# A triangular inverse kept as compact 32x32 diagonal blocks in the RWKV-7 stage of a decoder trunk

## The chip, the core and the metric

The kernel runs on one core of a Trainium2 chip. Its engines are TensorE (PE in the profile; PEld is its weight load), VectorE (DVE), ScalarE (ACT), GpSimd (POOL) and SyncE (SP, which issues most DMAs). The metric is the device time of one execution in microseconds.

## The reference

Two decoder layers run over a prompt of 256 tokens and over 8 sample tokens, each with an FFN, a mixer of three parallel groups (RWKV-7, a short convolution, Mamba-2), and another FFN. The change is in the RWKV-7 group, whose recurrence per head is

```python
def step(S, inp):
    r_t, w_t, k_t, v_t, kk_t, b_t = inp
    Sa = jnp.einsum('bhij,bhj->bhi', S, -kk_t)
    S = S * w_t[:, :, None, :] + Sa[..., None] * b_t[:, :, None, :] + v_t[..., None] * k_t[:, :, None, :]
    return S, jnp.einsum('bhij,bhj->bhi', S, r_t)
```

for 16 heads of width 64. The kernel computes it for the prompt in chunks of 64 tokens. Within a chunk the rank-one updates depend on one another through a strictly triangular 64x64 matrix N, so that a chunk needs the inverse of I - N (signs as the kernel takes them). The 8 sample tokens take one plain step each.

## The kernel before

`back_stage` does this part once in each of the two layers. Two heads lie on the 128 partitions, so there are 8 head pairs (RT = 8). With 4 chunks there are 8 triangular 64x64 matrices to a pair: 4 along the free axis (index q) in each partition half.

A hand-written software pipeline runs over steps g = 0 to 9. In step g the pair g gets its products (`gram`, then `mask` on DVE, and on POOL `first_done`, the first level of the inverse), the pair l = g - 1 gets its inverse, and the pairs c = g - 2 and p = g - 3 get `solve`, `transfer`, `own_outputs`, `own_states`, `chunk`, and the mean and variance. Each engine runs its own list in program order. Semaphores join the lists: nothing else sets the order.

The inverse is grown by doubling. X (`x`, tile `inverse`) and its transpose (`xt`, tile `inverse_t`) are right for diagonal blocks of size b, and a level makes them right for 2b: `levels` masks the off-diagonal blocks of N (`level` on POOL, tile `n_levels`), TensorE forms T1 = N_b X (`level_t1`), ACT copies T1 from PSUM (`t1_copy`, tile `n_x`), TensorE forms X T1 and its transpose (`level_u`, two products), and DVE adds both to `x` and `xt` (`update`). The levels are 2, 4, 8, 16 and 32, and the last needs only the transpose. A product here (`blocks`) is 8 matmuls of a 64x64 weight block with 64 columns, in fp32; the trace has two records for each fp32 matmul, 16 to a product. The halves of the partitions are separate array tiles. Before level 0 DVE adds the identity to `xt` (`start`), TensorE transposes it (`turn_x`), and ACT copies that to `x` (`x_copy`). `solve` uses `xt` as the weights.

DVE also runs the eight instructions of the sample step (`step`), two to `mask` the next pair, `transfer`, `centre` and `gated`. In the last steps PE and DVE take work for the output projection as well (`short`, `ws.split_lo`). The lists between them are those of the functions below.

## Time and profile before

| | |
|---|---|
| median of 3 runs | 1665.74 us (1665.28 to 1670.03) |
| span of the profiled execution | 1667.1 us |
| granted TensorE clock, mean over the span | 0.983 |
| PE busy | 1566.2 us (94%) |
| DVE busy | 1140.1 us (68%) |
| ACT busy | 858.5 us (51%) |
| POOL busy | 262.7 us (16%) |
| back_stage's loop in layer 0 (g = 0 to 9), roughly | 441 to 597 us |
| the same in layer 1, roughly | 1261 to 1419 us |

The profile is of one execution, and no time of its own stands beside its span; the span is 1.4 us above the median of the runs. A busy share says how long an engine had at least one instruction in flight: matmuls overlap, so PE can be at 94% and still have room.

### The profile page before, as it was taken

The page shows a single profiled execution, that of the slowest core. Times are in us where ns is not written, and L with a number is a line of the kernel's source. Part 1 is how long each engine was busy: PE and PEld are TensorE (multiplying, and loading weights), DVE is VectorE, ACT ScalarE, POOL GpSimd, SP SyncE. Part 2 cuts the span into 40 slices and gives each one's busy share as a digit, 9 for nine tenths or more (in the row PEclk, how much of TensorE's full clock was granted, in tenths as well). Part 3 has the DMA queues.
Part 4 walks back from the last instruction along what each step waited for, and adds up shares of the span by engine and source line. Part 5 has one row for each costly group of instructions (what it writes and reads, how often), then busy time and mean ns, then how long its engine had stood idle before and what let it go on. Part 6 is the DMA issues. An engine that isn't in the chain of part 4 may idle for free. (4 is left out here: it accounts for less than half of the span.)

```text
span 1667.1 us, 41414 instructions
## 1 busy us (share of the span) xinstructions
PE 1566.2 (94%) x17379; PEld 1486.8 (89%) x17379; DVE 1140.1 (68%) x1822; ACT 858.5 (51%) x1515; POOL 262.7 (16%) x259
## 2 busy tenths in 40 slices
PE   7999999989799899999999999999997989899997
PEld 6999999987688789999999999989775878799997
DVE  6565587795798667665575656968768886676654
ACT  5444464667444555444354444657673445554443
POOL 0000003001356431000000000030014554300000
PEclk9999999999899999999999999999998999999999
DMA  7555556471244545555454655644703463455552
GB/s 230 178 172 170 168 159 199 130 208 53 59 125 120 144 157 161 194 179 186 143 186 160 194 183 175 189 141 128 215 1 102 126 178 98 131 189 187 183 178 71
DMA packets 280650, 256.28 MB, mean 154 GB/s; under 512 B 48054, under 2 KB 268700, under 8 KB 280450
## 3 DMA queue, kind: packets, MB, share of 16 engines
q1 hardware_dynamic: 276698, 252.05, 48.5%
q8 instruction: 139, 2.28, 0.6%
q10 hardware_dynamic: 3768, 1.59, 0.4%
q14 instruction: 45, 0.37, 0.1%
HBM read 242.22 MB, written 11.38 MB: 152 GB/s over the span
## 5 line engine op out<-in xcount | busy, mean ns | idle before, releaser
L209 ACT ACTIVATE front_hi<-front_raw 128x1024 fp32r<-128x1024 f32 (+2 forms) x230 | 238.5, 1039 | 262.0 <-PE ps L234 255.5
L216 DVE TENSOR_TENSOR front_lo<-front_raw,front_hi 128x1024 fp32r<-128x1024 f32 (+1 forms) x210 | 252.2, 1201 | 109.0 <-ACT front_hi L209 108.2
L209 ACT ACTIVATE out_hi<-out_raw 128x1024 fp32r<-128x1024 f32 (+1 forms) x168 | 173.3, 1038 | 219.1 <-PE ps L234 205.1
L216 DVE TENSOR_TENSOR out_lo<-out_raw,out_hi 128x1024 fp32r<-128x1024 f32 (+1 forms) x148 | 183.9, 1243 | 108.1 <-ACT out_hi L209 107.3
L232 PE MATMUL ps<-front_h_hi,front_hi 128*128 128x264 f32 (+1 forms) x816 | 241.3, 296 | 4.9 <-DVE front_lo L216 3.3
L234 PE MATMUL ps<-front_h_hi,front_lo 128*128 128x264 f32 (+1 forms) x816 | 233.0, 286 | 0.0
L233 PE MATMUL ps<-front_h_lo,front_hi 128*128 128x264 f32 (+1 forms) x816 | 232.7, 285 | 0.0
L232 PE MATMUL ps<-ffn_h_hi,out_hi 128*128 128x264 f32 x704 | 200.7, 285 | 0.1
L233 PE MATMUL ps<-ffn_h_lo,out_hi 128*128 128x264 f32 x704 | 200.0, 284 | 0.0
L234 PE MATMUL ps<-ffn_h_hi,out_lo 128*128 128x264 f32 x704 | 199.8, 284 | 0.0
L232 PE MATMUL ps<-in_h_hi,front_hi 128*128 128x264 f32 x688 | 197.4, 287 | 0.0
L234 PE MATMUL ps<-in_h_hi,front_lo 128*128 128x264 f32 x688 | 196.5, 286 | 0.0
L233 PE MATMUL ps<-in_h_lo,front_hi 128*128 128x264 f32 x688 | 196.5, 286 | 0.0
L232 PEld LDWEIGHTS ps<-front_h_hi,front_hi 128*128 128x128 f32 (+1 forms) x816 | 154.1, 189 | 13.5 <-issue 12.7
L233 PEld LDWEIGHTS ps<-front_h_lo,front_hi 128*128 128x128 f32 (+1 forms) x816 | 154.2, 189 | 0.7
L234 PEld LDWEIGHTS ps<-front_h_hi,front_lo 128*128 128x128 f32 (+1 forms) x816 | 153.5, 188 | 0.1
L216 POOL TENSOR_TENSOR front_lo<-front_raw,front_hi 128x1024 fp32r<-128x1024 f32 (+1 forms) x20 | 50.1, 2504 | 543.9 <-ACT front_hi L209 543.9
L232 PEld LDWEIGHTS ps<-ffn_h_hi,out_hi 128*128 128x128 f32 x704 | 132.7, 189 | 0.4 <-ACT ffn_h_hi L283 0.2
L233 PEld LDWEIGHTS ps<-ffn_h_lo,out_hi 128*128 128x128 f32 x704 | 132.7, 188 | 0.1
L234 PEld LDWEIGHTS ps<-ffn_h_hi,out_lo 128*128 128x128 f32 x704 | 132.6, 188 | 0.0
L233 PEld LDWEIGHTS ps<-in_h_lo,front_hi 128*128 128x128 f32 x688 | 131.3, 191 | 0.1
L232 PEld LDWEIGHTS ps<-in_h_hi,front_hi 128*128 128x128 f32 x688 | 131.2, 191 | 0.1
(400 smaller groups left out, 3891.7 us busy)
## 6 DMA issues: line engine op xcount, KB each, us to landing
front_raw<-in_w_in SPq DMA_DIRECT2D x50, 1024.0 KB, 5.2
out_raw<-in_ffn_w_in SPq DMA_DIRECT2D x44, 1024.0 KB, 5.2
front_raw<-in_ffn_w_in SPq DMA_DIRECT2D x40, 1024.0 KB, 5.3
back_sample_rows<-row_scratch SPq DMA_DIRECT2D x160, 128.0 KB, 3.0
out_raw<-in_w_out SPq DMA_DIRECT2D x16, 1024.0 KB, 6.3
front_raw<-in_ffn_w_out SPq DMA_DIRECT2D x16, 896.0 KB, 4.6
out_raw<-in_ffn_w_out SPq DMA_DIRECT2D x16, 896.0 KB, 4.6
front_raw<-in_ffn_w_out SPq DMA_DIRECT2D x8, 1024.0 KB, 5.0
```

Source lines behind the costliest of these rows:

```text
L209: act.activation(self.hi[n % self.RING][:, 0:k, 0:w], self._raw(n), ACT.Copy).then_inc(self.hi_ready, 1)
L216: eng.tensor_tensor(self.lo[n % self.RING][:, 0:k, 0:w], self._raw(n), self.hi[n % self.RING][:, 0:k, 0:w].bitcast(F32), ALU.subtract).the ...
L232: pe.matmul(out, hi[:, j, 0:w], x_hi[:, j], start=start and j == 0, stop=False)
L233: pe.matmul(out, hi[:, j, 0:w], x_lo[:, j], start=False, stop=False)
L234: mm = pe.matmul(out, lo[:, j, 0:w], x_hi[:, j], start=False, stop=stop and j == k - 1)
```

## The change

`x` now holds only the diagonal 32x32 blocks, one to each of the four partition quadrants, so a tile is 128x128 in place of 128x256. There are four levels (2 to 16) that work on these blocks, and a last step for the off-diagonal 32x32 block (LT = 5 steps in all). The products of the four levels (`small_blocks`) are 16 matmuls of a 32x32 weight block with 32 columns, on the four diagonal 32x32 tiles of the array. The transpose is no longer updated by a product of its own. After each change of `x`, DVE writes the transpose of each 32x32 block to `x_t` (`turn_blocks`), and waits for its own addition before. The last step is two half products (8 matmuls each). `finish` on DVE writes the right half of `xt`, `upper_blocks` on ACT the left half. `turn_x` no longer waits for DVE; DVE's addition of the identity (`start`) has moved from the middle of a step to its end and reads PSUM, and ACT's `x_copy` is gone. POOL loses one of five `level` operations a pair and gains one memset a layer.

```diff
--- before.py
+++ after.py
@@ -45,7 +45,8 @@
...
 LN_SCALE = 2.0 ** 20
-LEVELS = (2, 4, 8, 16, 32)
+LEVELS = (2, 4, 8, 16)
+HB = 32
 ROWS_A = (("norm_mix", 8), ("norm_ffn2", 8), ("rwkv_mu", 27), ("rwkv_w0", 8), ("rwkv_a0", 8),
@@ -77,6 +78,8 @@
...
     parts["levels"] = np.concatenate([level_t(b) for b in LEVELS], 1) * 1.0
+    parts["eye32"] = (i[:, None] % HB == np.arange(HB)[None, :]) * 1.0
+    parts["sides"] = np.stack([i % C < HB, i % C >= HB], 1) * 1.0
     t = np.arange(T)
...
@@ -1585,7 +1588,7 @@
-    LV, V = len(LEVELS), 5
+    LV, LT, V = len(LEVELS), len(LEVELS) + 1, 5
     KK, DEC, MB, KEY, REC = range(V)
...
@@ -1601,7 +1604,7 @@
...
         lev = st.sb("n_levels", [P, 2, 4, C])
-        x = st.sb("inverse", [P, 2, 4, C])
+        x, x_t = st.sb("inverse", [P, 2, 4, HB]), st.sb("inverse_blocks_t", [P, 2, 4, HB])
         xt = st.sb("inverse_t", [P, 3, 4, C])
...
@@ -1626,7 +1629,10 @@
...
         first, levels = env.const("first"), env.const("levels")
+        eye32, sides = env.const("eye32"), env.const("sides")
         half = (slice(0, C), slice(C, P))
+        quarter = tuple(slice(i * HB, (i + 1) * HB) for i in range(4))
+        in_block = (slice(0, HB), slice(HB, C))
         sin = d["state_rwkv_wkv"][layer].rearrange("b (m h) i j -> m (h i) b j", h=2)
...
@@ -1748,6 +1754,7 @@
...
                     pool.tensor_tensor(short_lo[:, c], mix.ys[:, c], short_hi[:, c].bitcast(F32), ALU.subtract).then_inc(s("short_lo"), 1)
+                pool.memset(t1[:, :, HB:C], 0.0).then_inc(s("t1_zeroed"), 1)
                 for g in range(RT + 1):
...
@@ -1770,7 +1777,6 @@
...
                     if l >= 0:
-                        level(l, 4)
                         key_row(l)
...
@@ -1800,15 +1806,15 @@
...
                 def t1_copy(p, i):
-                    n = LV * p + i
+                    n = LT * p + i
                     act.wait_ge(s("t1_ps"), n + 1)
                     if n:
-                        act.wait_ge(s("ut_ps"), n)
-                    act.activation(t1[:].rearrange("p q t -> p (q t)"), ps[:, T1B, 0:4 * C], ACT.Copy).then_inc(s("t1_in"), 1)
-
-                def x_copy(p):
-                    act.wait_ge(s("x_ps"), p + 1)
-                    act.activation(x[:, p % 2].rearrange("p q t -> p (q t)"), ps[:, T1B, 0:4 * C], ACT.Copy).then_inc(s("x_in"), 1)
+                        act.wait_ge(s("u_ps"), n)
+                    act.activation(t1[:, :, 0:HB], ps[:, T1B, 0:4 * HB].rearrange("p (q t) -> p q t", q=4), ACT.Copy).then_inc(s("t1_in"), 1)
+
+                def upper_blocks(p):
+                    act.wait_ge(s("xt_in"), LT * (p + 1))
+                    act.activation(xt[:, p % 3, :, 0:HB], x_t[:, p % 2], ACT.Copy, scale=sides[:, 0:1]).then_inc(s("upper_in"), 1)
                 def rv_copy(p):
...
@@ -1944,6 +1950,7 @@
...
                         t1_copy(l, 4)
+                        upper_blocks(l)
                         rv_copy(l)
...
@@ -1954,8 +1961,6 @@
...
                         shift_store(6)
-                    if g < RT:
-                        x_copy(g)
                     if c >= 0:
...
@@ -1999,24 +2004,28 @@
...
                                       cau[:].unsqueeze(1).to_broadcast([P, 4, 2 * C]), ALU.mult).then_inc(s("masked"), 1)
+                four = lambda b: ps[:, b, 0:4 * HB].rearrange("p (q t) -> p q t", q=4)
+                flat = lambda a: a.rearrange("p q t -> p (q t)")
+
+                def turn_blocks(p):
+                    dve.transpose(flat(x_t[:, p % 2]), flat(x[:, p % 2])).then_inc(s("xt_in"), 1)
+
                 def start(p):
-                    dve.wait_ge(s("first_done"), p + 1)
-                    dve.tensor_tensor(xt[:, p % 3], xt[:, p % 3], eye2.unsqueeze(1).to_broadcast([P, 4, C]),
-                                      ALU.add).then_inc(s("start"), 1)
+                    dve.wait_ge(s("x_ps"), p + 1)
+                    dve.tensor_tensor(x[:, p % 2], four(T1B), eye32.unsqueeze(1).to_broadcast([P, 4, HB]), ALU.add).then_inc(s("x_in"), 1)
+                    dve.wait_ge(s("x_in"), p + 1)
+                    turn_blocks(p)
                 def update(p, i):
-                    four = lambda b: ps[:, b, 0:4 * C].rearrange("p (q t) -> p q t", q=4)
-                    if i < LV - 1:
-                        dve.wait_ge(s("u_ps"), (LV - 1) * p + i + 1)
-                        if i:
-                            dve.wait_ge(s("x_up"), (LV - 1) * p + i)
-                        else:
-                            dve.wait_ge(s("x_in"), p + 1)
-                        dve.tensor_tensor(x[:, p % 2], x[:, p % 2], four(UB), ALU.add).then_inc(s("x_up"), 1)
-                    dve.wait_ge(s("ut_ps"), LV * p + i + 1)
-                    if i:
-                        dve.wait_ge(s("xt_up"), LV * p + i)
-                    dve.tensor_tensor(xt[:, p % 3], xt[:, p % 3], four(UB + 1), ALU.add).then_inc(s("xt_up"), 1)
+                    dve.wait_ge(s("u_ps"), LT * p + i + 1)
+                    dve.tensor_tensor(x[:, p % 2], x[:, p % 2], four(UB), ALU.add).then_inc(s("x_up"), 1)
+                    dve.wait_ge(s("x_up"), LV * p + i + 1)
+                    turn_blocks(p)
+
+                def finish(p):
+                    dve.wait_ge(s("u_ps"), LT * (p + 1))
+                    dve.scalar_tensor_tensor(out=xt[:, p % 3, :, HB:C], in0=x_t[:, p % 2], scalar=sides[:, 1:2], in1=four(UB + 1),
+                                             op0=ALU.mult, op1=ALU.add).then_inc(s("xt_up"), 1)
                 def transfer(p):
...
@@ -2105,8 +2114,6 @@
...
                         gated(p)
-                    if g < RT:
-                        start(g)
                     if g < 4:
...
@@ -2118,9 +2125,11 @@
...
                         step(l, 5)
-                        update(l, 4)
+                        finish(l)
                         step(l, 6)
                         step(l, 7)
+                    if g < RT:
+                        start(g)
                     if g == RT - 1:
...
@@ -2183,39 +2192,52 @@
...
                     mm.then_inc(s("g_ps"), 1)
-                def blocks(at, left, right):
+                def small_blocks(at, left, right):
                     for q in range(4):
-                        for w in half:
-                            mm = pe.matmul(ps[w, at, q * C:(q + 1) * C], left[w, q], right[w, q], start=True, stop=True)
+                        for i, w in enumerate(quarter):
+                            mm = pe.matmul(ps[w, at, q * HB:(q + 1) * HB], left(w, q, in_block[i % 2]), right(w, q), start=True, stop=True)
                     return mm
                 def turn_x(p):
-                    pe.wait_ge(s("start"), p + 1)
+                    pe.wait_ge(s("first_done"), p + 1)
                     if p:
-                        pe.wait_ge(s("t1_in"), LV * p)
-                    for q in range(4):
-                        for w in half:
-                            mm = pe.matmul(ps[w, T1B, q * C:(q + 1) * C], xt[w, p % 3, q], eye2[w], start=True, stop=True)
-                    mm.then_inc(s("x_ps"), 1)
+                        pe.wait_ge(s("t1_in"), LT * p)
+                    small_blocks(T1B, lambda w, q, c: xt[w, p % 3, q, c], lambda w, q: eye32[w]).then_inc(s("x_ps"), 1)
                 def level_t1(p, i):
                     n = LV * p + i
-                    pe.wait_ge(s("lev_done"), n + 1)
                     if i:
-                        pe.wait_ge(s("x_up"), (LV - 1) * p + i)
-                        pe.wait_ge(s("t1_in"), n)
+                        pe.wait_ge(s("x_up"), n)
+                        pe.wait_ge(s("t1_in"), LT * p + i)
                     else:
                         pe.wait_ge(s("x_in"), p + 1)
-                    blocks(T1B, lev[:, n % 2], x[:, p % 2]).then_inc(s("t1_ps"), 1)
+                    if i < LV:
+                        pe.wait_ge(s("lev_done"), n + 1)
+                        mm = small_blocks(T1B, lambda w, q, c: lev[w, n % 2, q, c], lambda w, q: x[w, p % 2, q])
+                    else:
+                        for q in range(4):
+                            for o in range(2):
+                                top, low = quarter[2 * o], quarter[2 * o + 1]
+                                mm = pe.matmul(ps[low, T1B, q * HB:(q + 1) * HB], gm[top, p % 3, q, 0, HB:C], x[top, p % 2, q],
+                                               start=True, stop=True)
+                    mm.then_inc(s("t1_ps"), 1)
                 def level_u(p, i):
-                    n = LV * p + i
-                    pe.wait_ge(s("t1_in"), n + 1)
-                    if n:
-                        pe.wait_ge(s("xt_up"), n)
-                    if i < LV - 1:
-                        blocks(UB, xt[:, p % 3], t1[:]).then_inc(s("u_ps"), 1)
-                    blocks(UB + 1, t1[:], xt[:, p % 3]).then_inc(s("ut_ps"), 1)
+                    pe.wait_ge(s("t1_in"), LT * p + i + 1)
+                    pe.wait_ge(s("xt_in"), LT * p + i + 1)
+                    if i < LV:
+                        mm = small_blocks(UB, lambda w, q, c: x_t[w, p % 2, q], lambda w, q: t1[w, q, 0:HB])
+                    else:
+                        if p == 0:
+                            pe.wait_ge(s("t1_zeroed"), 1)
+                        else:
+                            pe.wait_ge(s("xt_up"), p)
+                        for q in range(4):
+                            for o in range(2):
+                                low = quarter[2 * o + 1]
+                                mm = pe.matmul(ps[half[o], UB + 1, q * HB:(q + 1) * HB], t1[low, q], x_t[low, p % 2, q],
+                                               start=True, stop=True)
+                    mm.then_inc(s("u_ps"), 1)
                 def gv(p):
@@ -2235,7 +2257,8 @@
                 def solve(p):
-                    pe.wait_ge(s("xt_up"), LV * (p + 1))
+                    pe.wait_ge(s("xt_up"), p + 1)
+                    pe.wait_ge(s("upper_in"), p + 1)
                     pe.wait_ge(s("rv_in"), p + 1)
```

In TensorE's list, the second half of step g = 3 (pair l = 2, from the products behind T1 of the fourth level). `back_inverse,back_n_levels` or `back_inverse,back_products` is a T1, L2299 and L2304 are `chunk`, L2232 is `gv`, L2198 before is `turn_x`. Before:

```order
L2189 MATMUL ps<-back_n_x,back_inverse_t 64x64 x8
L2189 MATMUL ps<-back_inverse_t,back_n_x 64x64 x8
L2299 MATMUL ps<-back_read_out,back_states 64x64 x2
L2304 MATMUL ps<-back_states,back_carry 64x64 x2
L2189 MATMUL ps<-back_inverse,back_n_levels 64x64 x8
L2232 MATMUL ps<-back_tok,back_products 64x64 x8
L2299 MATMUL ps<-back_read_out,back_states 64x64 x2
L2304 MATMUL ps<-back_states,back_carry 64x64 x2
L2189 MATMUL ps<-back_inverse_t,back_n_x 64x64 x8
L2198 MATMUL ps<-cst,back_inverse_t 64x64 x8
```

The same stretch of TensorE's list now (L2322 and L2327 are `chunk`, L2254 is `gv`):

```order
L2198 MATMUL ps<-back_n_x,back_inverse_blocks_t 32x32 x16
L2322 MATMUL ps<-back_read_out,back_states 64x64 x2
L2327 MATMUL ps<-back_states,back_carry 64x64 x2
L2221 MATMUL ps<-back_inverse,back_products 32x32 x8
L2254 MATMUL ps<-back_tok,back_products 64x64 x8
L2322 MATMUL ps<-back_read_out,back_states 64x64 x2
L2327 MATMUL ps<-back_states,back_carry 64x64 x2
L2238 MATMUL ps<-back_inverse_blocks_t,back_n_x 64x32 x8
L2198 MATMUL ps<-cst,back_inverse_t 32x32 x16
```

The order of the work is the same. Of the two products behind a T1 one is gone, the others have twice the matmuls at a quarter of the size, and tiles of 32 and of 64 now alternate.

In DVE's list, the end of step g = 4 and the begin of the next, before (`back_prod` and the rows with `back_sample` are the sample step, `back_products` the masks):

```order
L2015 TENSOR_TENSOR back_inverse<-back_inverse,ps 128x256
L2019 TENSOR_TENSOR back_inverse_t<-back_inverse_t,ps 128x256
L2068 SCALAR_TENSOR_TENSOR gate_211<-xs,cols,gate_211 128x264
L2004 TENSOR_TENSOR back_inverse_t<-back_inverse_t,cst 128x256
L2052 TENSOR_TENSOR back_sample_wkv<-back_sample_wkv,back_outer 128x512
L2019 TENSOR_TENSOR back_inverse_t<-back_inverse_t,ps 128x256
L2055 TENSOR_TENSOR back_prod<-back_sample_wkv,back_sample_rows 128x512
L2057 TENSOR_REDUCE xs<-back_prod 128x8
L1998 TENSOR_TENSOR back_products<-ps,cst 128x512 x2
```

and now:

```order
L2021 TENSOR_TENSOR back_inverse<-back_inverse,ps 128x128
L2011 STREAM_TRANSPOSE back_inverse_blocks_t<-back_inverse 128x128
L2077 SCALAR_TENSOR_TENSOR gate_211<-xs,cols,gate_211 128x264
L2061 TENSOR_TENSOR back_sample_wkv<-back_sample_wkv,back_outer 128x512
L2027 SCALAR_TENSOR_TENSOR back_inverse_t<-back_inverse_blocks_t,cst,ps 128x4x32
L2064 TENSOR_TENSOR back_prod<-back_sample_wkv,back_sample_rows 128x512
L2066 TENSOR_REDUCE xs<-back_prod 128x8
L2015 TENSOR_TENSOR back_inverse<-ps,cst 128x128
L2011 STREAM_TRANSPOSE back_inverse_blocks_t<-back_inverse 128x128
L2003 TENSOR_TENSOR back_products<-ps,cst 128x512 x2
```

`start` (L2004 before, L2015 and L2011 now) stands behind the whole sample step, right ahead of the masks of the next pair.

In step g = 0, DVE's list before:

```order
L2004 TENSOR_TENSOR back_inverse_t<-back_inverse_t,cst 128x256
L2112 SCALAR_TENSOR_TENSOR bonus_212<-bonus_212,cols,gate_211 128x264 x2
L2117 SCALAR_TENSOR_TENSOR y_short<-y_short,cols,sc_root_219 128x264 x3
L1998 TENSOR_TENSOR back_products<-ps,cst 128x512 x2
L2015 TENSOR_TENSOR back_inverse<-back_inverse,ps 128x256
```

and now, with five vector operations ahead of `start`:

```order
L2119 SCALAR_TENSOR_TENSOR bonus_212<-bonus_212,cols,gate_211 128x264 x2
L2124 SCALAR_TENSOR_TENSOR y_short<-y_short,cols,sc_root_219 128x264 x3
L2015 TENSOR_TENSOR back_inverse<-ps,cst 128x128
L2011 STREAM_TRANSPOSE back_inverse_blocks_t<-back_inverse 128x128
L2003 TENSOR_TENSOR back_products<-ps,cst 128x512 x2
```

Here `start` has moved behind `bonus` and `y_short`, and both of its instructions work on 128 elements in place of 256.

## Rows read from the trace of the kernel before

**Rows 1.** The page's head, part 1 and the clock line of part 2.
```profile
span 1667.1 us, 41414 instructions
...
PE 1566.2 (94%) x17379; PEld 1486.8 (89%) x17379; DVE 1140.1 (68%) x1822; ACT 858.5 (51%) x1515; POOL 262.7 (16%) x259
...
PEclk9999999999899999999999999999998999999999
```

**Rows 2.** Busy us (instructions) by engine, clock, DMA; stretches are steps 2 to 7.
```profile
467.31:481.36 14.05, 12.79 (x420) 11.83 (x416) 13.48 (x26) 6.12 (x18) 9.61 (x11) 1.00 0.48 134
...
543.90:561.54 17.64, 13.75 (x394) 12.23 (x389) 13.00 (x24) 8.17 (x23) 10.85 (x10) 1.00 0.95 268
sum 94.23, PE 86.25 PEld 77.87 DVE 80.17 ACT 42.01 POOL 56.37; mean PE 14.38 PEld 12.98 DVE 13.36 ACT 7.00 POOL 9.39
```

**Rows 3.** Who waited for whom over those six steps, engines of the loop.
```profile
DVE back_inverse L2015 <- PE ps L2189: 7.2, 14, 1.6
PE ps L2189 <- issue: 4.7, 5, 2.9
```

**Rows 4.** Timeline, one level of pair 3 (start us, us, what; x counts records).
```profile
500.18 0.68 PE L2189 MATMUL ps<-back_n_x,back_inverse_t 64*64 64x64 f32 x16
500.70 0.63 PE L2189 MATMUL ps<-back_inverse_t,back_n_x 64*64 64x64 f32 x16
500.91 0.42 DVE L2015 TENSOR_TENSOR back_inverse<-back_inverse,ps 128x256 f32<-128x256 f32 x1
501.26 0.66 PE L2167 MATMUL ps<-cst,back_b_k 128*128 128x128 f32 x4
501.38 0.42 DVE L2019 TENSOR_TENSOR back_inverse_t<-back_inverse_t,ps 128x256 f32<-128x256 f32 x1
501.72 0.68 DVE L2041 TENSOR_REDUCE back_sample_sa<-back_prod 128x8 f32<-128x512 f32 x1
```

**Rows 5.** Timeline of PE, step g = 9: products whose matmuls lie on four 64x64 tiles.
```profile
591.22 0.46 PE L2275 MATMUL ps<-back_products,back_tok 64*64 64x64 f32 x16
591.50 0.41 PE L2279 MATMUL ps<-back_products,back_u_w 64*64 64x64 f32 x16
591.73 0.41 PE L2286 MATMUL ps<-back_tok 64*64 64x64 f32 x16
```

**Rows 6.** Instructions of L2189 (ns min/median/max), and groups by line of L739 and L740.
```profile
L2189 PE MATMUL ps<-back_inverse,back_n_levels x1280: 212/219/268, 449.5 to 1402.0; 64*64 64x64 f32 x183
...
L739 PE MATMUL ps<-cst,fin_squares_sum 128*128 128x1 f32 x4 | 0.5, 230 | 0.0
...
L740 PE MATMUL ps<-cst,fin_squares_sum 128*8 128x1 f32 x2 | 0.2, 168 | 0.0
```

**Rows 7.** Groups by line with shapes kept apart (count | busy us, mean ns).
```profile
L1998 DVE TENSOR_TENSOR back_products<-ps,cst 128x512 f32<-128x512 f32 x32 | 20.5, 682 | 10.9 <-PE ps L2182 10.9
...
L1216 DVE SCALAR_TENSOR_TENSOR segments<-ps,tok_cum_dt,cst 128x128 f32<-128x128 f32 x16 | 5.5, 341 | 0.0
...
L796 DVE TENSOR_TENSOR xbc_conv<-xbc_conv,outer 128x64 f32<-128x64 f32 x6 | 1.4, 225 | 0.2
```

**Rows 8.** Timeline of DVE in step g = 0 and into g = 1, layer 0.
```profile
445.39 0.89 DVE L2004 TENSOR_TENSOR back_inverse_t<-back_inverse_t,cst 128x256 f32<-128x256 f32 x1 [0.84 <-POOL back_inverse_t L1759]
...
447.86 2.67 DVE L2117 SCALAR_TENSOR_TENSOR y_short<-y_short,cols,sc_root 128x264 f32<-128x264 f32 x3
450.45 1.27 DVE L1998 TENSOR_TENSOR back_products<-ps,cst 128x512 f32<-128x512 f32 x2
```

**Rows 9.** Timeline of PE in step g = 8, after the projection's first matmuls.
```profile
571.50 0.62 PE L2189 MATMUL ps<-back_inverse,back_n_levels 64*64 64x64 f32 x14
...
582.87 1.09 PE L2243 MATMUL ps<-back_gv_a,back_inverse_t 64*64 64x128 f32 x16
```

**Rows 10.** Timeline of PE in step g = 7, a wait inside a product.
```profile
558.31 0.27 PE L2189 MATMUL ps<-back_inverse_t,back_n_x 64*64 64x64 f32 x3 [2.86 <-issue]
```

**Rows 11.** Busy time by stretch at the loop's start in layer 1.
```profile
1257.00:1273.00 16.00, 12.44 (x202) 9.76 (x204) 9.66 (x14) 7.02 (x17) 7.86 (x10) 0.79 0.45 120
```

6 lines of the change are left out of this document (3 added, 3 removed).

## The prediction

> **What bounds the kernel now.** I read the page first: the span is 1667.1 us, PE is busy for 94% of it and its clock is granted almost throughout [rows 1]. The chain that ended last is PE nearly everywhere, which says little about a pipelined loop, so I went on to the stage that the change touches and cut it at the first mask of each pipeline step. Six steps, g = 2 to 7, take 94.23 us, 15.7 each; in a step PE is busy for 14.38, DVE for 13.36, ACT for 7.0 and POOL for 9.4 [rows 2]. So two engines are close to the bound and neither is it alone. The list of waits says the same: in six steps DVE waits 7.2 us for PE ahead of `x`'s update, and PE waits 4.7 us for "issue", 2.9 of it in one place [rows 3, 10]. The two in-order lists interlock. Relief of one engine alone is worth less than it measures; here both get some, of unequal size, and a step should shrink by an amount between the two.
>
> **PE's products.** A product of 16 records starts 0.52 us after the one ahead of it (500.18 and 500.70) [rows 4]; I take 0.5. A pair has 15: one for `turn_x`, five T1, four for `x`, five for `xt`, so 7.5 us. One record lasts 0.22 [rows 6], so the other 15 start within 0.68 - 0.22 = 0.46, 31 ns apart, on two array tiles: 62 ns between records on one tile. Products that use four tiles start 0.28 and 0.23 apart [rows 5], 16 ns a record, again some 62 ns on one tile. So a tile accepts a record about every 62 ns when it has 64 columns behind a 64-wide weight, tiles work side by side, and records can be issued 16 ns apart at least. Does a tile's pace shrink with the size? Four records with 128-wide weights and one column took 0.50, two with 8-wide weights 0.20, of which the last record is 0.17 (the mean) [rows 6]: 0.03 apart. So it shrinks, down to 0.03 at least. A 32x32 record has half the columns and half the weights: I take 31 ns a tile. A small product is 32 records on four tiles, 8 rounds, 0.25 us. The bounds: 0.25 below, since nothing shows a tile under 30 ns, and above 32 x 31 ns = 1.0, if they got only the pace of the two-tile products. A choice of 0.5 would be the 16 ns a record that four tiles do show. I take 0.25 because the tile, and not the issue, sets the pace in both rows that I have.
>
> A pair then has nine small products (2.25), a T1 of 16 records on two tiles (0.25) and a last product whose weights are 64 wide (0.5): 3.0 in place of 7.5, 4.5 us less.
>
> **Changes of tile size.** The last record of the product that starts at 500.70 starts at 501.33 - 0.22 = 501.11, the first 128x128 record at 501.26: 0.15 later, where inside a product it is 0.03 [rows 4]. The first record behind a change is also 0.05 longer (268 against 219) [rows 6]. I take 0.15 for a change. From PE's list, a step now changes between 64 and 128 six times; after the change every product of the inverse stands between others, and there are 21 changes. Fifteen more cost 2.25 us. Net, PE gets 2.25 us a step back. The Trainium skill (TensorEngine Tiling (Array Packing), Key Properties) says that a change of tiling mode drains the engine. The trace agrees with 0.15 us, and with a free change the relief would be 4.5.
>
> **DVE.** The update of `x` holds DVE for 0.47 (500.91 to 501.38) and that of `xt` for 0.34 (to 501.72) [rows 4]; three levels at 0.81, one at 0.66 (I take 0.33 for each operation where no wait splits them), the last `xt` and `start` at 0.34 each make 3.8 us. Now there are five additions of 128 elements, each awaited by the transpose behind it, five transposes, and `finish`. A 64-element operation takes 0.225 and a 256-element one 0.42, so 128 elements 0.29; with the semaphore 0.32 for the awaited one and 0.21 for one followed by a stranger (0.08 less than its duration, as 0.34 against 0.42). `finish` is like the 128-element operation from PSUM at 0.341, 0.26 in the queue [rows 4, 7]. That is 5 x 0.53 + 0.26 = 2.9, so 0.9 less. No row shows a block transposition. Below, it can't beat 0.225 (saving 0.3 more a pair); above I take the 512-element mask, 0.68, which costs 5 x 0.39 = 1.95 more and turns the 0.9 into a loss of 1.05. I take 0.29, since it moves the same elements as the addition beside it. The Trainium skill (VectorE: DVE Perf Modes, The three transpose paths) gives 311 ns for 128x128 in bf16, an estimate for fp32 of 0.31; no run here shows it, and it would change the sum by 0.1.
>
> **The order.** The transpose is off the chain of a level: T1 needs only `x`, and T1 with ACT's copy (0.45 and 0.4) covers the 0.32 until `x_t` is there. ACT has room for `upper_blocks` [rows 2]. `start` now ends a step. PE then waits with `level_t1(l, 0)`, and behind it in its list stand `solve`, so `uw_copy` and `transfer`, and `level_u`. But PE has `turn_x`, `chunk` and `gram` (some 1.9 us) to do while DVE does `finish`, two sample instructions and `start` (some 1.9), and DVE has two masks (1.2) to do while PE catches up with T1 and `solve` (some 2). I charge 0.2 a step. In g = 0 `start` stands behind five instructions; they no longer stand behind the old `start`, its wait of 0.84 us for POOL and its 0.8 in the queue, so they end about 1.6 us before 450.45, at 448.8, early enough for the first T1 at 449.5. I count nothing there [rows 6, 8]. POOL's memset and its dropped level are off the path.
>
> **The sum.** A step gets shorter by something between DVE's 0.9 and PE's 2.25. The middle is 1.6, less 0.2 for the order: 1.4. Seven steps (g = 1 to 7) give 9.8. In g = 8 the chain of four levels from 571.50 to `solve` at 582.87 is 11.4 us [rows 9]: a level loses two times 0.25 on PE, 0.08 on ACT and 0.13 on DVE and gains two changes, 0.3, so 0.4 a level, 1.6. That is 11.4 a layer and 22.8 for both. The profile's span of 1667.1 lies 1.4 above the median of the runs, 1665.7; I subtract from the median: **1643 us**, and 1628 to 1655 for this case alone (a step 0.6 to 2.2 shorter).
>
> **Rivals.**
> - *More* (8%): DVE had its waits only because PE was late, and PE's full 2.25 comes through: 7 x 2.25 + 2.5, twice, 1629. For it speaks that DVE waits 7.2 us in six steps; against it, that DVE's busy 13.4 less 0.9 leaves 12.5.
> - *Little* (22%): the step is held by DVE's list and by the new wait at its end, where PE stands still, and it shrinks by 0.3: 7 x 0.3 + 0.8, twice, 1660. For it speaks the step of 14.05 us with DVE busy for 13.48 [rows 2].
> - *Small matmuls are dear* (9%, slower): 32x32 records get no four-way overlap and run 31 ns apart, a product costs 1.0. Then PE has 9 x 1.0 + 1.0 + 2.25 = 12.25 for 7.5, 4.75 more, of which its slack of 1.3 hides some: 3.4 a step, 16 steps, 55 us, 1720. It decides from 0.5 a product, where PE gains nothing, and certainly from 0.64. Against it speak the four-tile rows [rows 5]. The Trainium skill (same tiling page, Instruction Overhead) says that a matmul has about 60 cycles of overhead, so that 1 column costs as much as 60. Taken for records in a row, 25 ns each, that would be 0.8 a product and about 1700; rows 5, at 16 ns a record, disagree.
> - *The transposition is dear* (7%, slower): at 0.68 DVE loses 1.05 a step, about 0.6 of it in the period: 16 x 0.6, 1676. It decides from 0.47, where 5 x 0.18 eat the 0.9.
> - *The clock* (4%, slower): with sparser matmuls the granted clock falls inside the loop, as in the stretch with 0.79 after DVE and PE had little work [rows 11], which is 3.4 us of clock in 16. Eight such spells undo the gain and more: 1670. Against it: a stretch with PE busy for only 13.75 of 17.64 kept 1.00 [rows 2].
> - *As forecast* (50%).
>
> **How the numbers follow.** About 0.3%, 5 us, can be told from no change. Faster by more: 50 + 8 and a third of *little*, 66%. Within: most of the rest of *little*, 13%. Slower: 9 + 7 + 4 and 1 of *little*, 21%. The range leaves out *dear matmuls* and the far end of *more*: 1625 to 1680.
>
> **What would show it.** Right: six steps in 84 to 89 us; 32x32 products in which 32 records start within 0.3 us; `STREAM_TRANSPOSE` near 0.3; about 0.15 between a 32 and a 64 record; DVE's own busy time in a step near 12.5, PE's idle time higher, the clock at 1.00. Wrong: products of 0.5 or more, changes of 0.3 or more (15 of them then cost the whole 4.5), a transposition over 0.4, a wait of PE over 1 us at the head of each step, or a clock under 1.00 in the loop. A stall inside a product that waits for nothing the profile shows, as the 2.86 us in g = 7 [rows 10], could grow with PE's 160 matmuls a pair in place of 120; I have no price for it.

## The result, and the profile after the change

The change makes the kernel slower: 1695.16 us median of four runs (1691.84 to 1698.14) against 1666.66 of before (now four runs, 1665.28 to 1670.03), a ratio of 1.0168 with a 95% interval of 1.015 to 1.0185. The profiled execution spans 1689.8 us.

The page's head, the clock line and the queues of instruction transfers, after:

```profile
span 1689.8 us, 43864 instructions
...
PE 1554.5 (92%) x18659; PEld 1455.8 (86%) x18659; DVE 1115.5 (66%) x1838; ACT 852.7 (50%) x1515; POOL 251.3 (15%) x245
...
PEclk9999999999889799999999999999997988999999
...
q8 instruction: 149, 2.44, 0.6%
```

Against [rows 1], every engine is busy for less (PE 12 us, DVE 25, ACT 6, POOL 11) in a span that is 23 us longer. What went up is PE's instructions: 1280 MATMULs and as many weight loads. The last row is one that I had not read before the prediction: the queue that carries instructions. Its row of before:

```profile
q8 instruction: 139, 2.28, 0.6%
```

Ten transfers and 0.16 MB more for 2560 PE instructions: a transfer is 16 KB and brings a block of 256 instructions.

Busy time by stretch after, steps g = 2 to 7, in the columns of [rows 2]:

```profile
466.68:483.21 16.53, 15.11 (x520) 12.70 (x513) 11.52 (x26) 5.94 (x18) 8.35 (x10) 0.71 0.43 116
483.21:502.05 18.84, 13.68 (x529) 10.89 (x525) 13.01 (x29) 6.58 (x21) 7.88 (x10) 1.00 0.38 104
...
537.59:557.62 20.03, 16.53 (x529) 13.53 (x528) 11.57 (x25) 6.69 (x20) 7.97 (x10) 0.76 0.36 99
557.62:579.35 21.73, 14.87 (x510) 11.98 (x509) 12.41 (x25) 9.21 (x24) 10.17 (x9) 0.75 0.77 230
sum 112.67, PE 89.84 PEld 72.64 DVE 72.57 ACT 41.31 POOL 50.62; mean PE 14.97 PEld 12.11 DVE 12.09 ACT 6.89 POOL 8.44
```

Six steps take 112.67 us where they took 94.23. The second row is the one to look at: full clock, PE busy for 13.68, DVE for 13.01, and yet 18.84 us. PE's timeline in that stretch, the rows with a wait for nothing that the profile shows:

```profile
484.29 0.39 PE L2198 MATMUL ps<-back_inverse,back_n_levels 32*32 32x32 f32 x24 [1.03 <-issue]
488.64 0.45 PE L2290 MATMUL ps<-back_products,back_u_w 64*64 64x64 f32 x12 [1.19 <-issue]
492.98 0.38 PE L2198 MATMUL ps<-back_n_x,back_inverse_blocks_t 32*32 32x32 f32 x20 [1.22 <-issue]
497.48 0.33 PE L2327 MATMUL ps<-back_states,back_carry 64*64 64x64 f32 x3 [1.21 <-issue]
501.56 0.44 PE L2191 MATMUL ps<-back_a_r,back_b_k 64*64 64x128 f32 x6 [0.32 <-issue]
```

PE stops in the middle of products, of old ones (`chunk`, the state products) as of new ones, at even distances. Cut from stop to stop:

```profile
484.28:488.63 4.35, 2.98 (x125) 2.35 (x125) 1.75 (x4) 1.42 (x4) 4.09 (x6) 1.00 0.42 104
488.63:492.97 4.34, 3.12 (x126) 2.44 (x126) 3.09 (x6) 0.87 (x2) 2.74 (x4) 1.00 0.19 65
492.97:497.47 4.50, 3.29 (x127) 2.52 (x127) 3.96 (x10) 1.62 (x6) 1.05 (x1) 1.00 0.30 97
```

125 to 127 MATMUL records and as many weight loads, with a few semaphore instructions: one transfer of 256 instructions each time. PE has used up a block and the next one is not there. Over the six steps the pace is the same before and after: some 2,550 records, 20.2 blocks, in 94.23 us are 4.7 us a block, some 3,090 records, 24.5 blocks, in 112.67 are 4.6. The equal pace does not say that the supply bound the kernel before, as the runs with few rows show below. Added up over the whole span, PE's waits for "issue" are 13.8 us before the change and 40.7 after. The 26.9 us more are nearly the whole loss of 28.5.

Not every wait for "issue" is one for a block, so I also counted PE's instructions (MATMULs, weight loads and semaphore instructions) in the packed traces. A block's end falls at every 256th instruction, always at the same remainder. Of the 40.7 us, 39.1 are 37 stops of 0.1 us or more that all stand within four instructions of such an end. Before the change there are 10 such stops with 9.3 us. In the trace after, transfer number k (from 0) never starts before PE has begun 256 k + 154 instructions, and PE never gets beyond 256 k + 449 until transfer k is over. So a transfer starts only when PE has fewer than 300 instructions left. PE resumes some 2.4 us after the start of the transfer that it lacked (median of the stops in the loops), though the transfer itself takes about 1.0.

One more wait grew in these six steps. PE waits three times for `start` (DVE's L2015) at the head of a step, up to 1.5 us (us in total, times, longest):

```profile
PE ps L2198 <- issue: 12.7, 9, 2.7
PE ps L2198 <- DVE back_inverse L2015: 3.0, 3, 1.5
```

The small products and the transposition themselves, after (the instructions of one line, ns min/median/max; then groups by line; then the timeline):

```profile
L2198 PE MATMUL ps<-back_inverse,back_n_levels x2048: 184/191/258, 450.9 to 1422.0; 32*32 32x32 f32 x187
```

```profile
L2011 DVE STREAM_TRANSPOSE back_inverse_blocks_t<-back_inverse 128x128 f32<-128x128 f32 x80 | 24.9, 312 | 2.7
```

```profile
486.51 0.45 PE L2198 MATMUL ps<-back_inverse,back_n_levels 32*32 32x32 f32 x32 [0.19 <-DVE back_inverse L2021]
486.89 0.46 PE L2287 MATMUL ps<-back_tok,back_u_w 64*64 64x64 f32 x16
```

All 32 records of a product start within 0.45 - 0.19 = 0.26 us, 8 ns apart, and the next tile size starts 486.89 - 486.77 = 0.12 behind the last. (The Trainium skill, TensorEngine Tiling (Array Packing), Instruction Overhead, gives a matmul some 60 cycles of overhead, an estimate of 25 ns. If that held for records in a row, whatever their tiles, the 8 ns here would disagree; on one tile a record comes every 34 ns, and there nothing in this trace contradicts it.)

### The profile page after: what moved, and what is told of

The parts are those of the page before. It is cut to its first block and busy times, and to the rows that moved or that the text cites. A ratio compares the mean times of both kernels' runs of the same rounds, so it can differ in the third digit from the quotient of the medians.

```text
span 1689.8 us, 43864 instructions
## 1 busy us (share of the span) xinstructions
PE 1554.5 (92%) x18659; PEld 1455.8 (86%) x18659; DVE 1115.5 (66%) x1838; ACT 852.7 (50%) x1515; POOL 251.3 (15%) x245
```

## The experiments

Three theories. **Supply**: PE's instructions come in blocks of 256, and in the loop a block takes 4.3 to 4.5 us where PE has to wait for it; 530 records a step are 4.2 blocks. **Clock**: the granted clock was 0.71 to 0.82 in some steps. **Order**: `start` at the end of DVE's list. All ratios are against the kernel before, with 95% intervals.

| run | us | ratio | the inverse's matmuls a pair | instruction transfers |
|---|---|---|---|---|
| after | 1695.2 | 1.0168 (1.015 to 1.0185) | 160 | 149 |
| T1 and `turn_x` merged | 1663.4 | 0.9975 (0.9959 to 0.9991) | 120 | 139 |
| before, weights split | 1692.4 | 1.0142 (1.0122 to 1.0161) | 160 | 149 |
| before, columns split | 1701.5 | 1.0199 (1.018 to 1.0219) | 160 | 149 |
| after, filled | 1703.4 | 1.0212 (1.0186 to 1.0237) | 160 + 6 | 150 |
| before, spread waits | 1692.5 | 1.0145 (1.0129 to 1.0162) | 120 | 142 |
| before, clustered waits | 1704.8 | 1.0214 (1.0198 to 1.0229) | 120 | 144 |
| merged, filled in g = 0 to 2 | 1671.7 | 1.0025 (1.0014 to 1.0036) | 120 + 6 | 139 |
| no `turn_x` | 1659.9 | 0.9945 (0.9926 to 0.9964) | 112 | 137 |
| the same, `start` at the end | 1665.4 | 0.9988 (0.9975 to 1.0001) | 112 | 137 |
| full blocks, transposed by DVE | 1652.1 | 0.9907 (0.9891 to 0.9922) | 88 | 131 |
| the same, `start` on POOL | 1659.6 | 0.9948 (0.9935 to 0.9962) | 88 | 131 |
| after, few rows | 1680.1 | 1.0066 (1.0043 to 1.0089) | 160 | 149 |
| before, few rows | 1665.0 | 0.9973 (0.9962 to 0.9985) | 120 | 139 |
| split, few rows | 1678.2 | 1.0062 (1.0047 to 1.0077) | 160 | 149 |
| merged, few rows | 1656.3 | 0.9931 (0.9914 to 0.9948) | 120 | 139 |
| clusters, few rows | 1700.1 | 1.0189 (1.0171 to 1.0206) | 120 | 144 |

Not all of the ranges recorded before the runs held. The weight split (1692.4) and the spread waits (1692.5) came out just below the supply theory's ranges, the filled merged kernel (1671.7) and `start` on POOL (1659.6) above every range given for them. The run without `turn_x` (1659.9) came out where neither of its theories had it. With few rows, the changed, the split and the merged kernel fell between the two ranges that each had. The clustered waits and the column split came out inside the supply theory's ranges, but for reasons of their own, as said below.

### Fewer instructions for the same work

The masked levels are block diagonal in 32s, so one 64x64 weight does what two 32x32 weights do:

```diff
-                        mm = small_blocks(T1B, lambda w, q, c: lev[w, n % 2, q, c], lambda w, q: x[w, p % 2, q])
+                        for q in range(4):
+                            for w in half:
+                                mm = pe.matmul(ps[w, T1B, q * HB:(q + 1) * HB], lev[w, n % 2, q], x[w, p % 2, q], start=True, stop=True)
```

> The changed kernel, with T1 of the four levels and turn_x as 8 matmuls of a 64x64 weight (block diagonal in 32s) with 32 columns in place of 16 matmuls of 32x32: the same result, PE's time much the same, but 120 matmuls a pair as before the change, not 160. Theory A (supply): PE takes its instructions in blocks of some 126 MATMUL records with their weight loads, and a block cannot take less than about 4.35 us. A step of the changed kernel has some 530 records, 4.2 blocks, 18.3 us (the measured mean of seven steps is 18.3); with 445 it is 3.5 blocks, 15.4 us. So seven steps take 105 to 112 us in place of 128, and the time falls to 1650 to 1668. Theory B (clock): the granted clock falls in the loop because matmuls are small and sparse; they stay so, so the steps stay near 18 and the time is 1685 to 1700. Theory C (the transposition and start at the end of DVE's list): nothing of it is changed, 1690 to 1697.

(`turn_x` is merged in the same way.) 1663.4, so 32 us go with 40 matmuls a pair, more than the whole loss of 28.5. PE's waits for "issue" are 15.0 us in all, of which 13.4 at ends of blocks, 25.7 less than after the change. The steps fall to 13.9 to 17.2, two of them:

```profile
464.88:481.14 16.26, 15.32 (x440) 13.41 (x438) 11.30 (x26) 5.97 (x18) 7.56 (x10) 0.72 0.44 117
481.14:495.79 14.65, 13.66 (x449) 11.34 (x445) 12.43 (x28) 6.61 (x21) 8.83 (x10) 1.00 0.49 133
```

The edit changes one more thing: T1 now has the tile size of its neighbours, so that a step changes tile size 14.8 times in this trace, where it was 20.7 after the change (5.7 before it). Six changes fewer at 0.12 are 0.7 us of PE's time a step, at most 11 us in 16 steps. No run separates them from the 40 matmuls; the 25.7 us less at ends of blocks leave some 6 of the 32 us for them.

### The same number of instructions in the kernel before

```diff
-                    blocks(T1B, lev[:, n % 2], x[:, p % 2]).then_inc(s("t1_ps"), 1)
+                    for q in range(4):
+                        for o, w in enumerate(half):
+                            for k in range(2):
+                                to = slice(o * C + k * 32, o * C + k * 32 + 32)
+                                mm = pe.matmul(ps[to, T1B, q * C:(q + 1) * C], lev[w, n % 2, q, k * 32:k * 32 + 32], x[w, p % 2, q],
+                                               start=True, stop=True)
+                    mm.then_inc(s("t1_ps"), 1)
```

> The kernel before, with each T1 of the inverse as 16 matmuls (weights of 64x32 in place of 64x64, the same columns): nothing else is changed, but a pair has 160 matmuls, as many as after the change. Theory A: a step goes from some 445 to some 525 records, 3.5 to 4.2 blocks of 4.35 us, so 15.7 to about 18.2 us, 16 steps, 1695 to 1710, with a stall inside a product about every 126 records. Theories B and C: the full-size products, VectorE's list and start are as before; only ten more changes of tile size come in, 1.5 us of PE's time a step of which its slack hides most, so 1666 to 1680, and no stalls at even distances.

> The kernel before, with each T1 as 16 matmuls of 64x64 weights with 32 columns in place of 8 with 64: no other tile size and no new change of tile size, but each weight is loaded twice, and a pair has 160 matmuls. Theory A: as the run with weights in halves, 1695 to 1710, stalls about every 126 records. Theories B and C: 1666 if 32 columns cost half of 64, up to 1685 if a matmul costs by its weight (5 x 0.5 us a step, less PE's slack of 1.3).

The second run splits the moving columns instead (`ps[w, T1B, at:at + 32]`, `x[w, p % 2, q, k * 32:k * 32 + 32]`). 1692.4 and 1701.5, with the clock at 1.00 in every step from g = 1 to 6 and neither a transposition nor a moved `start`. Two steps of the first, and a block between two of its stops:

```profile
482.35:499.84 17.49, 15.97 (x528) 13.62 (x517) 13.57 (x27) 7.46 (x22) 8.64 (x11) 1.00 0.38 106
499.84:518.59 18.75, 16.02 (x514) 13.74 (x518) 12.71 (x25) 7.18 (x21) 8.44 (x11) 1.00 0.43 114
...
500.21:504.59 4.38, 3.79 (x125) 3.29 (x126) 2.38 (x5) 1.64 (x4) 3.39 (x5) 1.00 0.49 125
```

125 records in 4.38 us again. But PE is also busier (16.0 a step), so part of these 24 us can be the array's. A step has 12.6 changes of tile size here, seven more than before the split, and the stops at ends of blocks grew by only 9 us (9.3 to 18.5). The runs with few rows below bear on it. In the column split PE is busy for 17.2 to 17.7 us a step: each weight is loaded twice, and that run says little of the supply.

### The clock

```diff
                     src = [b_k(p)[:, 0], b_k(p)[:, 1]] if part == 0 else [v[:, p], a_r(p)[:, 0]]
+                    for _ in range(3):
+                        pe.matmul(ps[:, GB + part, 0:4 * C], ident, levels[:, 0:4 * C], start=True, stop=True)
```

> The changed kernel, with six idle matmuls a step (128x128 weights, 256 columns, fp32, written to a bank that the transposes behind them overwrite): 24 more instructions and about 3 us more of PE's time a step, at places where PE has some 4 us of idle time. Theory B: with more columns the clock stays at 1.00 in the loop, and since the steps at a lower clock (0.71 to 0.83) make up most of the loss, the time falls to 1665 to 1680. Theory A: the supply sets the step, and 24 instructions are 0.1 of a block: the clock rises but the time stays, 1690 to 1705, with the stalls where they were.

```profile
486.86:506.30 19.44, 15.87 (x553) 12.70 (x556) 12.24 (x27) 6.73 (x21) 8.39 (x10) 1.00 0.32 92
506.30:523.51 17.21, 15.27 (x554) 12.53 (x543) 11.58 (x26) 6.84 (x21) 7.97 (x10) 1.00 0.43 114
523.51:540.84 17.33, 15.85 (x548) 12.86 (x534) 12.46 (x27) 6.73 (x21) 7.79 (x10) 1.00 0.41 113
540.84:558.88 18.04, 15.61 (x543) 12.83 (x532) 12.16 (x27) 6.11 (x19) 7.90 (x10) 1.00 0.37 111
```

With the filler the clock is at 1.00 in these four steps (g = 3 to 6; after the change two of them had 0.82 and 0.76) and they stayed at 17.2 to 19.4 us; the time rose by 8. The two steps that had had a lower clock took 1.8 and 2.0 us less than without the filler, the two at 1.00 0.6 and 0.8 more, so the clock may hold a part in single steps, which the filler's own time hides. It is not the cause of the loss: the merged kernel wins back all of it with a mean granted clock of 0.969 over the span, hardly above the change's 0.964 (0.983 before), and the weight split loses 24 us at 1.00. The same filler on the merged kernel, in g = 0 to 2 alone:

> The changed kernel with T1 in 64x64 weights (1663), and six idle matmuls of 256 columns in each of the steps g = 0, 1 and 2 alone, where its granted clock was 0.94, 0.85 and 0.72. 72 more instructions in a layer. If a step at a low clock costs what the clock says, the clock rises to 1.00 there and the two layers gain 2 to 6 us: 1657 to 1661. If the clock there hides behind other waits: 1663 to 1668, by the filler's own 3 us a step.

It cost 8 us as well (1671.7), more than either range: in those steps the filler's own time is more than the clock gives back.

### Instructions that are no matmuls

`pe.wait_ge(s("vecs_ps"), 1)`, satisfied since the loop's start, once or twice ahead of each matmul of `blocks`, and then twelve times ahead of each call of it:

> The kernel before with 168 more instructions a pair that are no matmuls: ahead of each matmul of the inverse's T1, x and xt products PE waits once or twice for a semaphore that has long been at its value. No matmul, operand or tile size is changed. Theory A, that PE's supply is counted in instructions (some 256 to a block of at least 4.35 us): 0.66 of a block a step, 2.8 us, 16 steps: 1668 goes to 1695 to 1715, with stalls inside products that now have fewer than 126 MATMUL records between them. If it is the number of matmuls or of weight loads that counts, or the array: 1668 to 1675.

> The kernel before with twelve waits in a row, for a semaphore long at its value, ahead of each of the 14 T1, x and xt products of a pair: some 155 instructions more a pair, no matmul and no operand changed. In the run with one or two waits ahead of each matmul only 56 of 168 came out as instructions of their own (the trace has 896 more), 3 blocks more, and the time rose by 25 us, 1.5 us a step, where 0.22 of a block is 1.0: so the supply is shown there, but a wait may also have a price of its own. Theory A: 0.6 of a block at 4.45 us a step, 2.7 us, 16 steps, 43 us: 1700 to 1718, nine or ten blocks more, and stalls 106 records apart (256 instructions at 920 + 155 to a step of 445 matmul records). If a wait has a large price of its own: 1725 or more, with the time in front of products and not at even distances. If instructions cost nothing: 1668 to 1675.

1692.5 and 1704.8. The trace has 896 and 1344 instructions more, 56 and 84 a pair. The first shows the block's content: between two stops there are now 117 records, where 256 x 445 / (920 + 56) = 117 would be (445 records of each kind and some 30 others a step before).

```profile
535.86:541.30 5.44, 4.18 (x117) 3.85 (x117) 2.78 (x5) 1.64 (x4) 3.35 (x5) 1.00 0.50 109
```

As a price of the supply they prove nothing, though: with few rows, the clusters still cost 35 us over the same kernel without them (1700.1 against 1665.0), and the stops at ends of blocks are 6.9 us there against 5.1. So it is the satisfied waits themselves that cost, by this estimate 35 / (16 x 84) = 26 ns for each.

### One part of the change alone, and `start`

The kernel before in full 64x64 blocks, where at levels 0 to 3 DVE's block transposition takes the place of the `xt` product and its addition:

```diff
...
                         dve.tensor_tensor(x[:, p % 2], x[:, p % 2], four(UB), ALU.add).then_inc(s("x_up"), 1)
-                    dve.wait_ge(s("ut_ps"), LV * p + i + 1)
...
-                    dve.tensor_tensor(xt[:, p % 3], xt[:, p % 3], four(UB + 1), ALU.add).then_inc(s("xt_up"), 1)
+                        dve.wait_ge(s("x_up"), (LV - 1) * p + i + 1)
...
+                        dve.transpose(flat(x_t[:, p % 2]), flat(x[:, p % 2])).then_inc(s("xt_in"), 1)
...
```

> One part of the change alone: the kernel before, with x and xt as full 64x64 blocks and all its 64x64 matmuls, but at levels 0 to 3 the transpose of x comes from VectorE's block transposition (128x256, into a tile of its own) and not from a product and an addition. 88 matmuls a pair where before it were 120 and after the change 160. Theory A: 380 records a step are 3.0 blocks, 13.2 us, so the supply no longer binds; VectorE (13.4 us of its own, four transpositions of perhaps 0.55 for four additions of 0.42, and a wait for its own addition each) then sets 14.0 to 14.8, 1640 to 1655. If the supply was not what bound the kernel before the change: VectorE's list was, and it grows, 1665 to 1680.

1652.1, the fastest of all, 0.9% under the kernel before. It does not tell the supply from the array: with 32 matmuls a pair fewer PE also has four products less to work on, and the stops at ends of blocks fell by only 2 us (9.3 to 7.4). Two of its steps, and the transposition of 256 elements:

```profile
511.37:525.89 14.52, 13.43 (x379) 11.72 (x377) 13.70 (x26) 7.12 (x22) 9.29 (x11) 1.00 0.48 133
525.89:540.40 14.51, 13.41 (x379) 11.74 (x376) 13.72 (x26) 6.52 (x20) 9.29 (x11) 1.00 0.47 132
```

```profile
L2016 DVE STREAM_TRANSPOSE back_inverse_now_t<-back_inverse 128x256 f32<-128x256 f32 x64 | 28.5, 445 | 2.2
```

DVE, busy for 13.7 of 14.5 us, is close to the bound now. I moved its addition of the identity to POOL:

> The full-block version with VectorE's transposition (1652), and the addition of the identity (start) moved from VectorE to POOL. In 1652 the supply no longer binds (2.9 blocks a step of 14.5 us) and VectorE is busy for 13.5 of 14.5 us. Theory: VectorE is the bound there, and 0.4 us less on it gives 0.3 a step: 1645 to 1650. If the chain of the levels or the remaining supply stalls hold the step: 1650 to 1656.

1659.6, a miss: PE's weight loads now wait 6.3 us for POOL's `n_levels` between 465 and 560 us (2.7 in the run before), in a loop where POOL got an addition of 0.8 us a step to do ahead of them.

In the compact version, without `turn_x` (POOL adds the column halves, DVE adds the identity and transposes), `start` in mid-step and then at the end:

> The changed kernel with T1 in 64x64 weights, as in the first of these runs (1663), and the product turn_x gone as well: POOL adds the two column halves of the first level (one of them is zero in each row), VectorE adds the identity to that and turns it into x, in the middle of the step where start stood before the change. 112 matmuls a pair, 32 instructions fewer. Theory A: 0.125 of a block less, 0.54 us a step, 1650 to 1657, until VectorE's 12.3 us and the chain between the engines bound it. Theory C (start at the end of VectorE's list holds the step): up to 1 us a step more, 1640 to 1650. If neither: 1660 to 1666.

> The version without turn_x (1660), with start moved back to the end of VectorE's list, where the change puts it. Theory C, that start there makes PE wait at the head of each step: 0.3 to 1 us a step, 1665 to 1676. Theory A: the blocks are the same in number, so the time is the same within what can be measured, 1657 to 1664.

1659.9 and 1665.4: the place at the end costs 5.5 us, 0.34 a step. PE waits for `x` there, 4.3 us in four steps of the second run.

### Does the supply share the DMA engines with data?

From the second pair on, the sample rows are loaded to 2 partitions of a half and not 64 (their values are wrong in the rest):

```diff
-                e.dma_start(rows[half[h], n].rearrange("p b j -> p (b j)"),
+                k = 2 if m else C
+                e.dma_start(rows[h * C:h * C + k, n].rearrange("p b j -> p (b j)"),
...
```

> The changed kernel (1695) with the loads of the sample rows cut from 64 to 2 partitions to a half from the second pair on (the rows of later pairs are then wrong in the other partitions; the same instructions and waits stay): the loop's data transfers fall from a third of the DMA engines' time to a few per cent. It asks what sets the time of a block of instructions. If the blocks wait behind data in the DMA engines: they come every 3.4 us, the least distance in any trace, and the steps fall towards 15 us, 1650 to 1670. If a block has a latency of its own: 1690 to 1698.

> The kernel before with the sample rows' loads cut to 2 partitions of 64 from the second pair on (the rows of later pairs are wrong in the other partitions). If it stood at the limit of the supply (3.4 blocks of 4.45 us a step), blocks of 3.6 us release it to what the engines allow, 14.4 to 15.0 a step: 1645 to 1660. If its limit was the engines alone: 1662 to 1670.

> The kernel before with T1 in 16 matmuls of 64x32 weights (1692, 160 matmuls a pair), and the row loads cut to 2 partitions of 64 as in the run beside it. Supply theory: 4.1 blocks of 3.6 us are 14.8 us, about what the engines need, so the 25 us that the split cost shrink to 0 to 10 above the run beside it. If the split cost its 25 us on the array (changes of tile size, more matmuls): it still costs 20 to 25.

> The changed kernel with T1 and turn_x in 64x64 weights (1663, 120 matmuls a pair), and the row loads cut likewise. Against the kernel before with the same cut it shows what the change does to the engines and the order when instructions are as many and their supply is fast. By the prediction's step, 1.4 us: 16 to 22 us less. If the order of the lists (start at the end) or the clock eats it: 0 to 8 less.

> The kernel before with twelve satisfied waits ahead of each T1, x and xt product (1705; 84 instructions more a pair), and the row loads cut likewise. If those waits cost by the supply alone: 3.9 blocks of 3.6 us are 14.1, under what the engines need, so 0 to 8 us over the kernel before with the same cut. If a wait has a price of its own on TensorE's queue: 20 to 37 over it.

The changed kernel gained 15 us, the split one 14, the merged one 7, the clusters 5, the kernel before 3. Two steps of the changed kernel with few rows, to hold against the 18.84 and 18.97 that these steps took with all rows:

```profile
482.08:496.71 14.63, 13.44 (x541) 10.76 (x529) 12.56 (x28) 6.60 (x21) 8.38 (x10) 1.00 0.19 43
496.71:511.35 14.64, 13.47 (x529) 10.70 (x519) 12.36 (x27) 6.60 (x21) 8.39 (x10) 1.00 0.21 48
```

Some 530 records in 14.6 us, a block every 3.5. So with less data in the DMA engines (a share of 0.38 and 0.40 in the slow steps, 0.2 here) blocks come every 3.5 us in place of 4.4. These are its best steps: g = 5 and 6 take 16.0 and 17.0 us at the same low share, and over 467 to 560 us the median distance of two transfers falls from 4.3 us to 3.8. The transfers themselves take as long as before (median 1.03 and 1.04 us in the loops) and PE resumes as long after their start (2.4 and 2.5); what shrinks is the time from PE's resuming to the start of the next transfer, 1.6 to 1.3 in the median.

The kernel before was hardly held by its supply on the mean (3 us). The split's 24 us shrank to 13, so about half was the supply behind data. The rest is not settled: its stops at ends of blocks are still 7 us above those of the kernel before (12.1 and 5.1), and its seven more changes of tile size a step, at 0.12 each, are up to 13 us of PE's time. Of the 32 us for 40 matmuls a pair, 24 stay with few rows (1680.1 - 1656.3): in later steps of that run PE still stops (31.8 us of "issue" in all, 30.2 at ends of blocks, where the merged one has 10.8). Transfers came no closer than 3.3 us in any of the 18 traces. That is about the least time from the start of a transfer to PE's resuming, 2.2, and the least from there to the next start, 1.1. What sets those two wasn't tried.

## Why the prediction was wrong

**The step that failed is the last sentence of the working**: that a stall inside a product, as the 2.86 us of [rows 10], could grow with 160 matmuls a pair, "I have no price for it". It was left out of the sum, the rivals and the range. In its place the runs show PE waiting for its next block of 256 instructions: 39.1 us at ends of blocks after the change, 9.3 before. The price could have been estimated from the trace: 0.6 of a block a step, 2.7 us, in 16 steps 43 less what engines would have hidden; measured, the 40 matmuls (with six changes of tile size a step) cost 32 us. The sum counted a matmul by the array's time for it, and by that measure four 32x32 matmuls cost no more than one of 64x64.

**PE's products** held: 0.26 us for the 0.25 forecast, 0.12 for the 0.15 of a change of size. **DVE's list** too: 312 ns for the 290 of the transposition, 285 for the 290 of the addition, 347 for `finish` (341); its busy time fell from 13.36 to 12.09 a step, 1.27 for the 0.9 forecast. The changes of tile size came out at 20.7 a step for the 21 counted. PE's busy time rose to 14.97 instead of falling, by stops that stretch the work and by steps at a lower clock.

**The middle of the two relieves, 1.4 a step,** was too large even without the supply: with few rows and equal counts, the merged version is 8.6 us faster than the kernel before (1656.3 against 1665.0), 0.5 a step. It is not quite the kernel of the forecast, since its T1 and `turn_x` are products of 64x64 weights. Of the missing 0.9, `start` at the end is 0.14: it cost 0.34 where 0.2 was charged, and a wait of PE over 1 us at the head of a step, of which the six steps have two (1.5 and 1.2), was among the signs that the prediction named. Another 0.36 are the stops at ends of blocks, which the merged kernel has even with few rows (10.8 us against 5.1). In g = 1 and 2 the merged kernel runs at a clock of 0.72 to 0.89, and the version without `turn_x` at 0.50 and 0.70, where the kernel before shows 1.00; the filler could not turn that into time, and the rest stays open.

**The rivals.** *Small matmuls are dear* (1720) was 25 us off; *the transposition is dear* (1676) was nearest in time, 19 us off, and did not happen. The first was right that their number costs, but wrong in place: not on the array, where a product takes 0.26 us. By its own working the 0.8 a product that it also names gives about 1690 and not 1700; that this is near the measured time is luck. *The clock* came true as an observation (0.71 to 0.83 in five of the steps g = 1 to 7 of layer 0) and false as the cause. The transposition took 312 ns and not 680; *little* and *more* did not happen. The range, 1625 to 1680, had its upper end from the clock and the transposition and no term for instructions. A smaller slip: a step shorter by 2.2 gives 1632, not the 1628 that stands for it; nothing hangs on it.

**What the trace of the kernel before would have told.** The stop of 2.86 us stands in a step whose DMA share is 0.95 [rows 2], and the page has a row for instruction transfers. Its transfers in the loop are 4.7 us apart on the mean, and none is closer than 3.6: at a step of 14.3 us, the forecast, 4.2 blocks would have had to come every 3.4.

## What to carry to other kernels

Count instructions as well as array time: a loop of small fp32 matmuls (two MATMULs and two weight loads each) can be bound by how fast its instructions arrive. "Issue" waits of an in-order engine in the middle of a product, at even counts of instructions, are the sign; the waits alone are not (the fastest kernel has 22 us of them, two thirds at other places). The time divided by the instruction queue's packets gives the pace, and here heavy data transfers beside it made it worse. Here a larger tile that holds two useful blocks and some zeros beat two exact small ones (1663 against 1695), and one vector instruction in place of a product of eight matmuls and an addition gave the fastest kernel (1652).

## What the hardware showed that I had not expected

- A transfer on the instruction queue holds 256 of PE's instructions. Where PE had to wait for them in step g = 3, one came every 4.3 to 4.5 us with data moving beside it, every 3.5 in the best steps with little of it, and in none of the 18 traces two under 3.3 apart. In the trace after, it starts only when PE has fewer than 300 instructions left, and after a stop PE resumes some 2.4 us from that start.
- Four 32x32 tiles take records 8 ns apart (32 in 0.26 us), one tile every 34.
- A block transposition of 128x128 fp32 takes 312 ns and one of 128x256 445, hardly more than the addition of that size (417).
- Semaphore waits that are already satisfied, twelve in a row, cost PE about 26 ns for each that came out as an instruction, by estimate. Of 168 such waits a pair, 84 did in rows of twelve and 56 singly or in twos.
